# Products put in another order on TensorE, and products of constants in front of waits, in a two-block diffusion layer on one core

## The reference, cut to what matters

```python
h  = modulate(rms_norm(x, g_mix), shift, scale)    # shift, scale = silu(c) @ w_mod + b_mod
px = split_columns(h @ w_in)                       # q_r k_r v_r g_r q_w k_w v_w q_n k_n v_n gates
ya = retention_mixer(px, pc)                       # q_r, k_r through axial_rope, then chunks of 128
yb = window_mixer(px, pc, sink)                    # q_w, k_w through axial_rope, band of 128
yc = na_mixer(px, pc, rpb)                         # q_n, k_n, v_n, 8 x 16 neighbours
x  = x + gate * ((ga*(ya@w_ret) + gb*(yb@w_win) + gc*(yc@w_na)) @ w_out)
x  = x + gate2 * expert_choice_ffn(modulate(rms_norm(x, g_ffn)), ...)
# second block, for l in (0, 1):
z  = split_columns_2((rmsnorm(x, pre_g) * (1 + scale) + shift) @ w_in)   # mod = silu(c) @ mod_w + mod_b
x  = x + gate * rmsnorm(merge_branches(z, mla(z), pool(z), gla(z)) , post_g)
```

## Time and profile before

| | us |
|---|---|
| median of 3 runs (lowest, highest) | 3061.38 (3058.29, 3069.1) |
| the profiled execution, its own time | 3058.66 |
| its span, first to last instruction | 3056.9 |
| PE busy with products | 2831.1 (93%) |
| DVE, ACT, POOL busy | 978.3, 898.1, 645.4 |
| mean granted TensorE clock | 0.955 |

### The profile page before, as it was taken

One profiled execution on the slowest core, in us unless ns is written; L12 is line 12 of the kernel. 1 busy time (PEld: TensorE's weight loads), 2 busy tenths in 40 slices (PEclk: granted clock), 3 DMA queues, 4 the chain that ended last, 5 costly groups with the idle time before them and its releaser, 6 DMA issues.

```text
span 3056.9 us, 37080 instructions
## 1 busy us (share of the span) xinstructions
PE 2831.1 (93%) x15238; PEld 2112.9 (69%) x15238; DVE 978.3 (32%) x1429; ACT 898.1 (29%) x1364; POOL 645.4 (21%) x323
## 2 busy tenths in 40 slices
PE   5899898999989999998999999999998988998997
PEld 3757677688754343347799667899996777576886
DVE  3332420621242111113166543211134065643113
ACT  4122333432331011103333244311124233343223
POOL 1212012044410000001221001522222231006443
PEclk8999999999989999998999999999997997999998
DMA  6143204022359999993122102111133121003222
GB/s 247 51 156 145 112 15 148 5 83 96 138 234 397 422 422 422 422 422 129 61 92 77 37 1 90 56 60 65 56 110 124 55 102 64 31 1 118 96 97 97
DMA packets 64784, 424.70 MB, mean 139 GB/s; under 512 B 6849, under 2 KB 6849, under 8 KB 18177
## 3 DMA queue, kind: packets, MB, share of 16 engines
q1 hardware_dynamic: 52416, 375.41, 31.3%
q0 software_dynamic: 3808, 27.81, 2.3%
q10 hardware_dynamic: 8416, 19.40, 1.7%
HBM read 405.56 MB, written 17.04 MB: 138 GB/s over the span
## 4 chain that ended last, share of the span: by engine, by line
PE 77%; DMA 9%; DVE 6%; ACT 5%; POOL 2%; issue 2%; ACTq 0%; SPq 0%; DVEq 0%; POOLq 0%
PE psum L670 73%; DMA ring<-in_weights 5%; PE psum L673 4%; DMA late_slots<-in_weights 2%; ACT hidden_high L1579 1%; POOL weight_parts L2788 1%; DMA arena<-in_t_count 1%; ACT arena L1588 1%; DMA residual<-in_acts 1%; DVE small L2115 1%; POOL arena L2881 1%; ACT hidden L1573 0%; ACT arena L1610 0%; DVE arena L2549 0%; POOL arena L2887 0%
## 5 line engine op out<-in xcount | busy, mean ns | idle before, releaser
L670 PE MATMUL psum<-hidden_high,weight_parts 128*128 128x384 f32 (+2 forms) x3296 | 875.4, 367 | 53.4 <-DVE hidden_low L2066 21.1
L2788 POOL TENSOR_TENSOR weight_parts<-ring,weight_parts 128x1024 fp32r<-128x1024 f32 x218 | 538.4, 2471 | 1362.0 <-ACT weight_parts L1543 1344.5
L670 PEld LDWEIGHTS psum<-hidden_high,weight_parts 128*128 128x128 f32 x3296 | 611.9, 193 | 133.2 <-issue 36.3
L670 PE MATMUL psum<-hidden_low,weight_parts 128*128 128x384 f32 (+2 forms) x2160 | 657.8, 365 | 4.8 <-DVE merged_low L2177 4.8
L1543 ACT ACTIVATE weight_parts<-ring 128x1024 fp32r<-128x1024 f32 x218 | 230.3, 1059 | 1093.6 <-PE psum L670 1081.0
L670 PE MATMUL psum<-arena 128*64 128x128 f32 (+8 forms) x3120 | 504.3, 368 | 21.8 <-DVE arena L2603 7.7
L670 PEld LDWEIGHTS psum<-hidden_low,weight_parts 128*128 128x128 f32 x2160 | 405.6, 192 | 44.6 <-DVE merged_low L2177 6.2
L670 PEld LDWEIGHTS psum<-arena 128*64 128x64 f32 (+3 forms) x3120 | 284.8, 162 | 180.8 <-issue 135.9
L1588 ACT ACTIVATE arena<-psum 128x512 f32<-128x512 f32 (+4 forms) x225 | 159.6, 720 | 394.5 <-PE psum L670 378.1
L2195 DVE TENSOR_TENSOR arena<-arena,psum 128x512 f32<-128x512 f32 (+1 forms) x72 | 55.9, 777 | 519.0 <-PE psum L670 518.2
L670 PE MATMUL psum<-ring,arena 128*64 128x512 f32 (+1 forms) x792 | 193.4, 600 | 14.4 <-DMA ring<-in_weights 12.6
(11 more groups left out here) (285 smaller groups left out, 2406.2 us busy)
## 6 DMA issues: line engine op xcount, KB each, us to landing
ring<-in_weights SPq DMA_DIRECT2D x260, 1024.0 KB, 6.8
late_slots<-in_weights SPq DMA_DIRECT2D x48, 1024.0 KB, 15.2
arena<-in_weights SPq DMA_DIRECT2D x48, 1024.0 KB, 17.4
spilled_projections<-arena ACTq DMA_DIRECT2D x14, 384.0 KB, 2.3
arena<-spilled_projections ACTq DMA_DIRECT2D x3, 1536.0 KB, 12.5
residual<-in_acts POOLq DMA_DIRECT2D x1, 3072.0 KB, 19.0
arena<-in_bias POOLq DMA_DIRECT2D x1, 3072.0 KB, 10.4
arena<-in_t_count POOLq DMA_DIRECT2D x2, 1536.0 KB, 9.8
```

The costliest lines, as they stand in the source:

```text
L670: return nc.tensor.matmul(o, lhsT, rhs, start=start, stop=stop)
L2788: G_.tensor_tensor(parts[:, i % 2, 1, :], tile_at(t), parts[:, i % 2, 0, :], ALU.subtract).then_inc(*E.sig("tile_split"))
```

## The change

In the order of the program:

- **Rotations.** The rotation of one q_r, k_r, k_w or q_w tile is issued among the projections of later tiles. To that end g_r is projected before v_r, and k_w before q_w, also in the stream plan and in the queues of ACT and DVE; on POOL, the load of the window tables goes in front of two weight splits.
- **Token groups.** `project_tokens` takes its three PSUM groups one after another in its first block, and ACT's `token_evac` copies out two of the three results before its fourth `high()`.
- **Two modulation rows** (`AMONG_TILES`) are summed in four steps each among the q_w tiles and the q_n, k_n tiles, into PSUM bank 6 and under semaphores of their own; ACT does not hold back its splits for them any more.
- **v_w** signals its end by a semaphore of its own.
- **Output tiles in step.** `w_out` runs its first two tiles together: blocks 0 to 5 of both, then blocks 6 and 7 of both.
- **Products of constants.** `keep_warm(n)` multiplies the identity by 256 columns of the constants into PSUM bank 6, n times, and nobody reads it. It stands in front of 24 waits, with 151 products in all.

The diff (cut to its core):

```diff
@@ stream_plan @@
-    out += rhs("w_in", (0,), "v_r", B1["v_r"], 512) + cols("w_in", (0,), "g_r", B1["g_r"], 4)
+    out += cols("w_in", (0,), "g_r", B1["g_r"], 4) + rhs("w_in", (0,), "v_r", B1["v_r"], 512)
...
+    out += cols("w_in", (0,), "k_w", B1["k_w"], 1)
+    out += q_w[0:1] + mod2(0, 0)[0:4] + q_w[1:3] + mod2(0, 0)[4:8] + q_w[3:4]
...
+    out += q_n[0:2] + mod2(0, 1)[0:2] + q_n[2:4] + mod2(0, 1)[2:4]
+    out += k_n[0:2] + mod2(0, 1)[4:8] + k_n[2:4]
@@ TensorE @@
+            def keep_warm(n):
+
+                for _ in range(n):
+                    mm(psum[:, 6 * 512:6 * 512 + 256], C("ident"), con[:, 0:256], True, True)
...
-                ps = [group(*name, p) for p in range(TT // 2)]
+                ps = []
...
+                            if k == 0 and t % 2 == 0:
+                                ps.append(group(*name, t // 2))
...
+                    if i == 0 and name[0] == "mla":
+                        keep_warm(4)
...
             def w_out(key, tiles, chunks):
-                for f in range(KT):
-                    project_tile(tiles(f), ("out", key, f), chunks, first=f == 0, src=(mHi, mLo),
-                                 ready="merged_parts")
+                both = []
+                for f in range(2):
+                    hi, lo = weight_parts(*tiles(f))
+                    both.append((split(hi, a=KT), split(lo, a=KT), group("out", key, f)))
+                    split_reader.append((psum_full, state["g"]))
+                    for k in range(KT - 2):
+                        out_products(*both[f], k, chunks, "merged_parts" if f == 0 else None)
+                for f in range(2):
+                    for k in range(KT - 2, KT):
+                        ins = out_products(*both[f], k, chunks, "merged_parts" if f == 0 else None)
+                    ins.then_inc(psum_full, 1)
+                    done()
...
+            def turned(kind, rot, src, t):
+                pe.wait_ge(*E.taken(kind, t))
+                rotations((kind,), rot, src, (t,))
+
             for t in range(4):
                 project_tile(("k_r", t), ("k_r", t), ALL)
...
+                if t:
+                    turned("q_r", C("rot_r"), lambda t: rQ[:, t, :], t - 1)
...
+            turned("k_w", C("rot_w"), lambda t: wK[:, CTX:TOK], 0)
+            pe.wait_ge(*E.next("cond2_ready"))
+            modulation_step(("mod2", 0), 0, cond2, range(0, 4))
+            project_tile(("q_w", 1), ("q_w", 1), IMG)
+            turned("q_w", C("rot_w"), lambda t: wQ[:, t, :], 0)
...
+                keep_warm(8)
                 pe.wait_ge(*E.next("head_squares", 2))
                 token_sums(("qn", l), [mSq[:, 0, :], mSq[:, 1, :]], OWN_CHUNKS[l])
@@ ScalarE @@
             def token_evac(name, dst):
 
-                for i in range(4):
+                for i in range(3):
                     high()
                 for p in range(TT // 2):
+                    if p == TT // 2 - 1:
+                        high()
                     evac((*name, p), dst[:, 2 * p:2 * p + 2, :].rearrange("p a n -> p (a n)"), n=1024)
...
+            high()
+            act.wait_ge(*E.next("window_values"))
+            act_(wV.rearrange("p a n -> p (a n)"), cols("v_w")[:, 0:TOK], ACT.Copy).then_inc(*E.read("v_w"))
...
             for t in range(4):
+                if t == 2:
+                    modulation_rows(("mod2", 0), 1)
                 high()
                 act.wait_ge(*E.written("k_n", t))
...
-            modulation_rows(("mod2", 0), 1)
-            high_again()
@@ GpSimd @@
-            low(20)
+            low(18)
...
             pool.dma_start(area(WIN + 3584, 1024), dram["t_win"]).then_inc(sem("win_tables_loaded"), 16)
+            low(2)
```

More of the change, by code:

```diff
@@ L775, in modulation_sums, with modulation_step @@
                 ins.then_inc(psum_full, 1)
+            def modulation_step(name, b, c, ks):
+                for k in ks:
+                    w = weights((name, b), k)
+                    for g in range(4):
+                        ins = mm(psum[32 * g:32 * g + 2, 6 * 512:6 * 512 + 256], c[:, k, :],
+                                 w[:, g * 256:(g + 1) * 256], k == 0, k == KT - 1)
+                        if g == 0:
+                            refill(ins)
+                    done()
+                if ks[-1] == KT - 1:
+                    ins.then_inc(sem("rows_summed"), 1)
             def modulation_turn(name, b, free=True):
-                pe.wait_ge(*E.taken(name, "row", b))
+                if (name, b) in AMONG_TILES:
+                    pe.wait_ge(*E.next("rows_taken"))
+                else:
+                    pe.wait_ge(*E.taken(name, "row", b))
                 ps = group(name, "column", b)
@@ L902, in branch_product, with merge @@
                 ins.then_inc(psum_full, 1)
-            def merge(key, chunks, ys, tags, src0=0, mixing=None):
+            def merge(key, chunks, ys, tags, src0=0, mixing=None, waits=(0, 0)):
                 def gates_of(f, b):
                     for g in (f, f + 1):
+                        if mixing and (b, g) in ((0, 0), (0, 1)):
+                            keep_warm(waits[g])
                         project_tile(("gate", *tags, b, g), ("gate", key, b, g), chunks)
@@ L998, in _ @@
                 modulation_sums("mod1", 2 + h, cond)
+                if h == 0:
+                    for p in range(TT // 2):
+                        pe.wait_ge(*E.taken("v_r", p))
                 ret_values(h)
@@ L1056, in _ @@
                 project_tile(("q_n", t), ("q_n", t), IMG)
+                if t == 0:
+                    for n in range(4):
+                        pe.wait_ge(*E.taken("R", "win", n))
+                if t % 2:
+                    modulation_step(("mod2", 0), 1, cond2, range(t - 1, t + 1))
             for t in range(4):
                 project_tile(("k_n", t), ("k_n", t), IMG_CHUNKS)
-            modulation_sums(("mod2", 0), 1, cond2)
+                if t == 1:
+                    modulation_step(("mod2", 0), 1, cond2, range(4, 8))
+                if t == 2:
+                    modulation_turn(("mod2", 0), 1)
             for t in range(4):
@@ L1481, in mixing @@
                     pe.wait_ge(*E.next("branches_ready", 4))
-                merge(("l", l), own, [YM, YP, YG], (l,), mixing=mixing)
+                merge(("l", l), own, [YM, YP, YG], (l,), mixing=mixing, waits=((0, 10), (7, 6))[l])
                 if l == 0:
@@ L1552, in modulation_rows @@
             def modulation_rows(name, b):
+                if (name, b) in AMONG_TILES:
+                    act.wait_ge(*E.next("rows_summed"))
+                    for g in range(4):
+                        ins = act_(modRow[name, b][0:2, g * 256:(g + 1) * 256],
+                                   psum[32 * g:32 * g + 2, 6 * 512:6 * 512 + 256], ACT.Copy)
+                    ins.then_inc(*E.sig("rows_taken"))
+                    return
                 act.wait_ge(*E.written(name, "row", b))
@@ L2313, in _ @@
             dve.wait_ge(*E.next("win_tables_loaded", 16))
-            for t in range(4):
-                rope(("q_w", t), wQ[:, t, :], wCos, wSin, wTmp[:, 0:512])
             rope(("k_w", 0), wK[:, CTX:TOK], wCos, wSin, wTmp[:, 0:512])
@@ L2320, in _ @@
             V.memset(wK[64:128, :], 0.0).then_inc(*E.sig("window_keys_padded"))
+            for t in range(4):
+                rope(("q_w", t), wQ[:, t, :], wCos, wSin, wTmp[:, 0:512])
             modulation_add(("mod2", 0), 0, modB[0], "bmod20")
```

97 lines of the change are left out of this document (63 added, 34 removed).

## The result

The changed kernel takes **3012.42 us** (median; 3010.27 to 3015.27) against 3061.24 us before: ratio 0.9835, 95% interval 0.9816 to 0.9853. The forecast was 2981 us with a range of 2963 to 3013. The direction is right, but of the 80 us forecast 49 came. The time lies 0.6 us inside the range, and two of the four runs (3014.2 and 3015.27) lie outside it; that the median falls inside is in part luck.

What follows compares the result with a forecast made beforehand. TensorE, filled with products for 93% of the span, was taken as the bound. Order 39.6 us plus constants 43.3 us, less 3 us for new waits, made 80 us off 3058.66 us: 2981 us as median, range 2963 to 3013 us.

Steps and rivals of the forecast that it cites:

- Rotations of q_r and k_r: Eight rotations waiting for `rope`, and the value products and wait behind them: the new order was to save 14.3 us.
- no gap over 0.3 us: Sign to look for: the eight rotations stand alone between tiles, with no TensorE gap longer than 0.3 us.
- Window stage: Stretch before the window attention's first score: 7.3 us saved, after 2.1 us of new wait for v_w's copy.
- Neighbourhood stage and v_n: Stretch before the neighbourhood attention, 2.8 us saved despite a new 3.0 us chain; waits around v_n, 3.1 us saved.
- Value tiles of layers 0 and 1: Two openings, two ends and three half-clock stretches at these tiles were to go: 13.7 us saved.
- Output tiles: Running the first two output tiles in step was to lose time at the third tile: -1.6 us together.
- The fill itself is nearly free.: At the 24 waits, 73.8 us long, the 151 products (69 us) cost almost nothing; their worth is the clock.
- Behind nine waits ... 24.8 us. I take all of it.: Dense products behind nine filled waits (latent attention, chunks, px, gates and others) return to full clock: 24.8 us saved.
- The narrow places: Five waits (decay twice, latent statistics twice, the end) before narrow or few-row products: 12 us saved, between 5 and 20.
- the starts: Three stage starts, where DVE paces the first tile: 6.5 us of 25.9 saved, between 2 and 12.
- Rival A: The products of constants run but do not hold the clock, so only the order counts: 3022 us, chance 0.08.
- rival B: The order gives half, with longer new waits at both attentions and the third output tile: 3001 us, chance 0.16.

Runs made afterwards that it cites:

- experiment 5: The changed kernel with the window table's transfer issued by POOL one split earlier (after 17 splits, not 18): 3004.04 us.
- experiment 6: The changed kernel with the output tiles one after the other again, `w_out` as in the kernel before: 3009.43 us.

## Why the prediction was right, and where it was not

The gain is 31 us short: 5.9 us are missing on the order and 28.1 on the constants, and against them stand the 3 us that the forecast had set aside for waits of this kind.

**The order: 33.7 us for 39.6.** Read from when the same ACT and DVE instructions start in the trace before and in that of the order alone:

- *Rotations of q_r and k_r (14.3).* 14.8 us at the end of v_r. Of these 1.7 go again, at a stretch of half clock behind the next wait (2.44 us, for a weight unit) that the trace before does not have there: sixteen matmuls of the modulation row take 1.89 us at 0.50 from 189.15 us on, and 1.04 us at 1.00 before, from 200.93 us on. Right, though "no gap over 0.3 us" holds only between the tiles: the last rotation, with nothing behind it but v_r, leaves 0.97 us.
- *Window stage (7.3).* 1.2 us, the step of the order that failed. I counted the wait for v_w's copy (2.11, forecast 2.1), but left out the table. I had let POOL's transfer stand as moved at no cost; in the new order it is needed right behind the first tile, not behind all six. With the table earlier (experiment 5) the place gains another 4.7 us, most of the term.
- *Neighbourhood stage and v_n (2.8 + 3.1).* 6.2 us; the new wait is 3.23 us, forecast 3.0.
- *Value tiles of layers 0 and 1 (13.7).* 7.2 + 7.9 us, a little more.
- *Output tiles (-1.6).* -1.8 in layer 0 at the place, -3.0 by the medians of experiment 6.

**The constants: 15.2 us for 43.3.** The mechanism held: the mean clock is 0.956 with the order alone and 0.974 with the constants, and the cost of the clock 106.4 and 65.9 us. At the first turn of latent attention, where 0.50 stood for 3.40 us behind a wait of 2.20 us, four plain products with the identity as an operand stand from 1727.15 us on, and the same 3.4 us behind them (from 1730.23 us) are at 1.00. The forecast counts half of PE's busy time at 0.50 as lost, 2.7 us of 5.48 for one. The products of constants bear this out (0.92 us against 0.465); the first matmuls of the chunks give a little less, (7.09 - 3.79) / 7.09 = 0.47. The failing steps are two:

- *"The fill itself is nearly free."* It was not: for 19 us of the 70 no idle time went. The step compared the length of the fill with waits taken from a trace in which PE also lost time at half clock. Once that time is gone the other engines' chains are late at the next place: chunk 4 (a new wait of 3.19 us), the third px tile and the second gate tile (waits of 2.13 and 2.64 us before, now 1.9 and 2.75 us of constants and then 2.42 and 2.47 us of wait). And where half clock came back, as in chunk 4, the next fill found no wait. I had asked what the fill costs at its own place only.
- *"Behind nine waits ... 24.8 us. I take all of it."* The runs without the other groups leave 15.2 - 4.3 - 8.4 + 0.7 = 3.2 us for the dense places other than px, gates and layer 0's end, where 24.8 - 3.0 - 3.1 = 18.7 were forecast. Four medians stand in this difference, so by my estimate it may be anything from nothing to some 9 us, still half of the forecast at most. Of the chunk loop's 9.6 us the change kept 1.5; filling chunk 4 too makes it 6.2, and the DVE's 14.5 us a chunk allow little more. Px and the gates (3.0) gave nothing against the kernel before, as POOL bounds the stage. Latent attention and the second merge gate of layer 0 did give most of what was forecast: by the starts of ACT's splits in the run with the constants alone, 1.3 us for 1.7 and 2.4 for 2.6. The narrow places (8.4 for 15 with layer 0's end) and the starts (4.3 for 6.5) were nearer, the two that I had discounted.

By the prediction's own signs: the mean clock went from 0.955 to 0.974, not 0.98; the chunks that were filled run at full clock, and half clock moved to the one between them. Rival A (3022 us, "the products of constants do not hold the clock") came nearest in time, 9.6 us off against 11.4 for rival B and 31 for the forecast, but neither is what happened: the constants took 40.5 us off the cost of the clock, and the order gave 33.7 of its 39.6 us. The range does not come out of its own terms either: 2981 - 15 and 3001 + 15 are 2966 and 3016 us, and it was put 3 us lower at both ends. The time lies in both.

How the 3.2 us divide among the other dense places stays open: differences of 1 to 2 us at one place lie under what untouched places show from run to run.

## What to carry to other kernels

A stall that is filled with dummy work, and slow time behind it that is cured, also hid other engines' work: go through the *next* waits with the new, earlier arrival of PE before counting the gain, and fill these too or use less. Check who is busy all through a stage before pricing its gaps. Where it is another engine (POOL 31.3 of 32 us, the DVE 13.5 of 14.5 us a chunk), the clock of PE is worth only what PE would take beyond it. When work is pulled forward, every input of it must be pulled forward too, the tables on another queue among them.

## What was not expected

The clock at the kernel's very start is not the same from run to run, with the same instructions. The stretch from 16.5 to 31.5 us, where PE waits for weights, before and with the order alone (the code there is the same):

```profile
16.50:31.50 15.00, 7.61 (x80) 2.71 (x72) 3.74 (x6) 6.71 (x11) 0.00 (x0) 1.00 1.00 414
```

```profile
16.50:31.50 15.00, 8.00 (x76) 2.88 (x72) 3.76 (x6) 6.72 (x11) 0.00 (x0) 0.50 0.99 411
```

Half the clock costs 0.4 us of busy time here, since the products wait for weights either way; but with the stretches at half clock behind it (35 to 66 us against 36 to 57) the q_r tiles come 2.9 us later. The price of a single gap has this spread between two executions, so I would forecast only sums over many gaps.

The window table's transfer took 8.1 us from issue to use where it ran beside weights, and 3.8 us when issued 6 us earlier. The DMA engines in that time, after, and in the run of experiment 5 (share and GB/s last):

```profile
272.00:276.00 4.00, 4.00 (x18) 3.29 (x18) 0.00 (x0) 0.00 (x0) 1.33 (x3) 1.00 0.88 363
276.00:280.00 4.00, 2.39 (x9) 1.31 (x7) 0.00 (x0) 0.00 (x0) 0.00 (x0) 1.00 1.02 426
```

```profile
266.00:270.30 4.30, 4.30 (x37) 2.51 (x38) 0.00 (x0) 1.54 (x2) 1.41 (x2) 1.00 0.35 122
```

So the late issue was paid twice here, once in its start and once in its length. That the weights' transfers made it longer is argued from these shares; no run takes them away.
